# The second feed-forward matrix by a seven-product 2x2 scheme, with the lower halves of the weight sums made by GpSimd

## What is computed

```python
        h = rmsnorm(x, norm_ffn[l])
        x = x + jnp.square(jax.nn.relu(h @ w_ff1[l])) @ w_ff2[l]
    return rmsnorm(x, final_norm)
```

## Time and profile before

| | |
|---|---|
| median of 3 runs | 1634.88 us (1634.79 to 1635.48) |
| span of the profiled execution | 1632.7 us |
| PE busy | 1612.9 us, 99% |
| DVE, ACT, POOL busy | 51%, 51%, 44% |
| mean granted clock of PE | 0.998 of full speed |
| the four passes | from about 526 to 874 us |

### The profile page before, as it was taken

One profiled execution on the slowest core, in us unless ns is written; L12 is line 12 of the kernel. 1 busy time (PEld: TensorE's weight loads), 2 busy tenths in 40 slices (PEclk: granted clock), 3 DMA queues, 4 the chain that ended last, 5 costly groups with the idle time before them and its releaser, 6 DMA issues.

```text
span 1632.7 us, 21256 instructions
## 1 busy us (share of the span) xinstructions
PE 1612.9 (99%) x7503; PEld 1331.9 (82%) x7503; DVE 836.2 (51%) x1278; ACT 828.1 (51%) x1109; POOL 710.5 (44%) x934
## 2 busy tenths in 40 slices
PE   7999999999999999999999999999999999999998
PEld 6888888888888888888887788888888887888886
DVE  3566666632114212121245957447447548688677
ACT  6467777743243413232346645444444446755675
POOL 7453333346666555555566535635635623000000
PEclk9999999999999999999999999999999999999999
DMA  7222221123333333333333222422322323332311
GB/s 209 78 83 60 64 77 58 46 71 110 90 116 91 103 91 103 91 102 92 103 90 90 78 65 77 116 65 75 115 69 65 116 65 92 92 92 69 106 64 62
DMA packets 249048, 142.93 MB, mean 88 GB/s; under 512 B 6162, under 2 KB 245523, under 8 KB 248979
## 3 DMA queue, kind: packets, MB, share of 16 engines
q1 hardware_dynamic: 248978, 142.00, 29.8%
HBM read 139.89 MB, written 2.10 MB: 87 GB/s over the span
## 4 chain that ended last, share of the span: by engine, by line
PE 78%; DVE 1%; issue 0%; ACT 0%; DVEq 0%
PE bank L806 21%; PE bank L807 20%; PE bank L814 20%; PE bank L797 2%; PE bank L799 2%; PE bank L798 2%; PE bank L1131 1%; PE bank L1112 1%; PE bank L1114 1%; PE bank L1113 1%; PE bank L1257 1%; PE bank L1259 1%; PE bank L1258 1%; PE bank L1164 1%; PE bank L1160 1%; PE bank L1162 1%
## 5 line engine op out<-in xcount | busy, mean ns | idle before, releaser
L777 POOL TENSOR_TENSOR w_lo<-raw,w_hi 128x256 fp32r<-128x256 f32 x896 | 699.5, 813 | 652.0 <-ACT w_hi L1364 651.5
L1364 ACT ACTIVATE w_hi<-raw 128x1024 fp32r<-128x1024 f32 x264 | 277.6, 1055 | 499.6 <-PE bank L814 453.6
L806 PE MATMUL bank<-h_hi,w_hi 128*128 128x512 f32 x1252 | 497.1, 397 | 0.0
L807 PE MATMUL bank<-h_lo,w_hi 128*128 128x512 f32 x1252 | 487.9, 390 | 0.0
L814 PE MATMUL bank<-h_hi,w_lo 128*128 128x512 f32 x1252 | 309.8, 389 | 0.0
L806 PEld LDWEIGHTS bank<-h_hi,w_hi 128*128 128x128 f32 x1252 | 235.1, 188 | 54.2 <-issue 6.0
L807 PEld LDWEIGHTS bank<-h_lo,w_hi 128*128 128x128 f32 x1252 | 235.1, 188 | 52.0 <-issue 4.1
L814 PEld LDWEIGHTS bank<-h_hi,w_lo 128*128 128x128 f32 x1252 | 235.0, 188 | 49.3 <-issue 0.5
L2202 DVE TENSOR_TENSOR xT<-xT,bank 128x512 f32<-128x512 f32 x102 | 67.5, 685 | 203.7 <-PE bank L814 159.6
L2227 DVE SCALAR_TENSOR_TENSOR fr<-bank,rstd 128x512 f32<-128x512 f32 x32 | 22.1, 691 | 132.5 <-PE bank L814 126.9
L806 PE MATMUL bank<-f_hi,w_hi 128*128 128x512 f32 x224 | 87.1, 389 | 0.0
(11 more groups left out here) (435 smaller groups left out, 2644.2 us busy)
## 6 DMA issues: line engine op xcount, KB each, us to landing
raw<-in_w_ff SPq DMA_DIRECT2D x64, 512.0 KB, 3.9
raw<-in_w_in SPq DMA_DIRECT2D x56, 512.0 KB, 3.7
raw<-in_m_w_in SPq DMA_DIRECT2D x48, 512.0 KB, 3.9
raw<-in_r_w_in SPq DMA_DIRECT2D x24, 512.0 KB, 3.8
raw<-in_m_w_out SPq DMA_DIRECT2D x16, 512.0 KB, 3.3
raw<-in_r_w_out SPq DMA_DIRECT2D x16, 384.0 KB, 3.0
raw<-in_w_up_b SPq DMA_DIRECT2D x8, 512.0 KB, 4.0
raw<-in_w_out SPq DMA_DIRECT2D x8, 512.0 KB, 4.0
```

Of the source, the lines that this page charges most:

```text
L777: ins = pool.tensor_tensor(w_lo[:, s, part], raw[:, s, part], w_hi[:, s, part].bitcast(F32), ALU.subtract)
L806: pe.matmul(dst, w_hi[:, s, c], hi[:, k, :], start=(k == 0), stop=False)
L807: pe.matmul(dst, w_hi[:, s, c], lo[:, k, :], start=False, stop=False)
L1364: act.activation(w_hi[:, p % RING, :], raw[:, p % RING, :], ACT.Copy).then_inc(hi_ready[p % RING], 1)
```

## The change

The second half of each pass is regrouped. The 2 x 2 blocks are: two output tiles of 128 (tiles 2c and 2c+1, "pair c", c = 0 to 3), two halves of the 1024 hidden units, and two halves of the 512 tokens. The scheme makes the four block products with seven multiplications of sums ("turns") instead of eight, each turn over 4 hidden tiles and 256 tokens.

- **PE** (`pair`): seven turns of 4 x 3 matmuls of 256 columns for each pair of panels, where there were 2 x 24 of 512. Turns add up in a bank (region 0 takes turns 0, 2, 4 and 6), so several values pass through it, and a turn waits until DVE has added the one before (semaphore chain).
- **DVE**: for each pair four weight sums of 128 x 512 in ss (`weight_sums`), made during the pair before it, those of pair 0 in the first half behind tile 4; seven adds of 256 columns from PSUM to xT; and in the first half differences of activation tiles (ft), with the lower halves of seven forms (`forms`). f_hi and f_lo hold seven forms x 4 hidden tiles x 256 tokens.
- **ACT**: per pair w_hi slots 0 (first panel), 1 and 2 (the sums, 1024 columns each) and 3 (half of the second panel), each once the turns that used it are done (`pair_upper`); in the first half the rounded forms in pieces. The copies of pair 0 stand among the squares of tiles 4 to 7: slot 3's comes behind all forms of tile 7.
- **POOL** (`pair_lower`): 14 pieces of 256 columns per pair where it made 8.
- **SP**: the raw slots of a pair are also released by DVE's sums (s_made). The first half's hidden tiles are taken in the order 0, 4, 1, 5, ...
- **The last pass**: the preparation of pair c's two tiles stands on DVE between the adds of pair c+1, one step behind each add; that of pair 3 behind everything. On ACT it stands behind the copies of the next pair's slots, for pair 3 behind the copies of the second block's first four panels.
- Some semaphores elsewhere are merged under new names, and a memset of gone moves from before the last pass to behind it.

```diff
+FORMS = 7
+NC = 4
+TURNS = [(0, 0, 0), (0, 1, 1), (1, 0, 4), (1, 1, 3), (2, 0, 5), (2, 1, 2), (3, 0, 6)]
+REGION = [0, 2, 0, 1, 0, 1, 0]
+CHAIN = 5
...
-        f_hi = sb("f_hi", [P, DT, S], F32R, a)
-        f_lo = sb("f_lo", [P, DT, S], F32R, a)
+        f_hi = sb("f_hi", [P, FORMS, NC, HALF], F32R, a)
+        f_lo = sb("f_lo", [P, FORMS, NC, HALF], F32R, a)
...
+        ft = sb("ft", [P, 4, HALF], F32, a)
+        ss = sb("ss", [P, 2, 4, S], F32, a)
...
+            def pair_lower(i, c):
+                one, two = 2 * c % RING, (2 * c + 1) % RING
+                at = (F_P + 8 + 2 * c) // RING + 1
+                pool.wait_ge(hi_ready[one], i * (F_N // RING) + at)
+                for q in range(PIECES):
+                    part = slice(q * QP, (q + 1) * QP)
+                    ins = lower(0, part, raw[:, one, part])
+                ins.then_inc(lo_ready[one], 1)
+                for s in (1, 2):
+                    pool.wait_ge(sum_hi, i * (2 * NC) + (2 * c + s))
+                    sums = ss[:, c % 2, 2 * s - 2:2 * s, :].rearrange("p a c -> p (a c)")
+                    for q in range(PIECES):
+                        part = slice(q * QP, (q + 1) * QP)
+                        ins = lower(s, part, sums[:, part])
+                        if q % 2:
+                            ins.then_inc(sum_lo_pool, 1)
+                pool.wait_ge(hi_ready[two], i * (F_N // RING) + at)
+                for q in range(2):
+                    part = slice(q * QP, (q + 1) * QP)
+                    ins = lower(3, part, raw[:, two, S + q * QP:S + (q + 1) * QP])
+                ins.then_inc(lo_ready[two], 1)
...
+            with pool.Fori(0, 4) as i:
+                for e in range(8):
+                    panel_lower(e % RING, i * (F_N // RING), (F_P + e) // RING + 1)
+                for c in range(NC):
+                    pair_lower(i, c)
...
+            def pair(i, c):
+                p, t = F_P + 8 + 2 * c, F_T + 8 + c // 2 * RING + c % 2
+                for n, (s, half, form) in enumerate(TURNS):
+                    dst = bank[[c % 2, 2 + c % 2, 5 + c % 2][REGION[n]]][:, 0:HALF]
+                    if n == 0:
+                        bank_ready(t, i, F_N)
+                        panel_split(pe, p, i, F_N)
+                    elif n == 2:
+                        pe.wait_ge(sum_lo_pool, i * (4 * NC) + (4 * c + 1))
+                        pe.wait_ge(chain, i * (CHAIN * NC) + (CHAIN * c + 1))
+                    elif n == 3:
+                        bank_ready(t + 2, i, F_N)
+                        pe.wait_ge(sum_lo_pool, i * (4 * NC) + (4 * c + 2))
+                    elif n == 4:
+                        pe.wait_ge(sum_lo_pool, i * (4 * NC) + (4 * c + 3))
+                        pe.wait_ge(chain, i * (CHAIN * NC) + (CHAIN * c + 3))
+                    elif n == 5:
+                        pe.wait_ge(sum_lo_pool, i * (4 * NC) + (4 * c + 4))
+                        pe.wait_ge(chain, i * (CHAIN * NC) + (CHAIN * c + 4))
+                    elif n == 6:
+                        panel_split(pe, p + 1, i, F_N)
+                        pe.wait_ge(chain, i * (CHAIN * NC) + (CHAIN * c + 5))
+                    for k in range(NC):
+                        if c == 0 and n in (0, 1, 2, 4):
+                            pe.wait_ge(f_made, i * (5 * NC) + (5 * k + {0: 1, 1: 3, 2: 4, 4: 5}[n]))
+                        at = slice(half * S + k * P, half * S + (k + 1) * P)
+                        pe.matmul(dst, w_hi[:, s, at], f_hi[:, form, k, :], start=(k == 0 and n in (0, 1, 3)),
+                                  stop=False, skip_group_check=True)
+                        pe.matmul(dst, w_hi[:, s, at], f_lo[:, form, k, :], start=False, stop=False,
+                                  skip_group_check=True)
+                        mm = pe.matmul(dst, w_lo[:, s, at], f_hi[:, form, k, :], start=False, stop=(k == NC - 1),
+                                       skip_group_check=True)
+                    mm.then_inc(turn_done, 1)
...
+            def pair_upper(i, c, before=None):
...
+                def free(turns, panel):
+                    if c:
+                        act.wait_ge(turn_done, i * (FORMS * NC) + (FORMS * (c - 1) + turns))
+                    else:
+                        tile_full(act, F_P + 4 + panel, i, F_N)
+                        if before:
+                            before(panel)
+                sums = ss[:, c % 2].rearrange("p a c -> p (a c)")
+                free(2, 0)
+                panel_loaded(act, p, i, F_N)
+                act.activation(w_hi[:, 0, :], raw[:, p % RING, :], ACT.Copy).then_inc(hi_ready[p % RING], 1)
+                free(4, 1)
+                act.wait_ge(s_made, i * (4 * NC) + (4 * c + 3))
+                act.activation(w_hi[:, 1, :], sums[:, 0:2 * S], ACT.Copy).then_inc(sum_hi, 1)
...
+                free(7, 3)
+                panel_loaded(act, p + 1, i, F_N)
+                act.activation(w_hi[:, 3, 0:S], raw[:, (p + 1) % RING, S:2 * S], ACT.Copy)\
+                   .then_inc(hi_ready[(p + 1) % RING], 1)
...
+                pair_upper(i, 0, lambda panel: squared(4 + panel))
+                for c in range(NC):
+                    if c + 1 < NC:
+                        pair_upper(i, c + 1)
+                    else:
+                        for panel in range(RING):
+                            act.wait_ge(turn_done, i * (FORMS * NC) + (FORMS * c + [2, 4, 6, 7][panel]))
+                            act.sem_inc(panel_done[panel], 2)
+                            upper(F_P + F_N + panel, i, F_N)
                     if last:
...
+            def weight_sums(i, c):
...
+                def first():
+                    panel_loaded(dve, p, i, F_N)
+                    panel_loaded(dve, p + 1, i, F_N)
+                    if c > 1 or not isinstance(i, int) or i > 0:
+                        dve.wait_ge(sum_lo_pool, i * (4 * NC) + (4 * c - 4))
+                    dve.tensor_tensor(to[:, 1, :], two[:, 0:S], two[:, S:2 * S], ALU.add).then_inc(s_made, 1)
+
+                def second():
+                    dve.tensor_tensor(to[:, 2, :], one[:, 0:S], two[:, 0:S], ALU.subtract).then_inc(s_made, 1)
+                def third():
+                    dve.wait_ge(s_made, i * (4 * NC) + (base_s + 1))
+                    dve.tensor_tensor(to[:, 0, :], to[:, 1, :], one[:, 0:S], ALU.subtract).then_inc(s_made, 1)
+                def fourth():
+                    dve.wait_ge(s_made, i * (4 * NC) + (base_s + 3))
+                    dve.tensor_tensor(to[:, 3, :], one[:, S:2 * S], to[:, 0, :], ALU.subtract).then_inc(s_made, 1)
...
+                def forms(e):
+                    c, z = e // 2, e % 2
+                    dve.wait_ge(ff_made, i * DT + (e + 1))
+                    if z == 0:
...
+                    else:
+                        dve.wait_ge(ft_made, i * (3 * NC) + (3 * c + 1))
+                        dve.tensor_tensor(ft[:, 1, :], ff[:, 1, HALF:S], ft[:, 0, :], ALU.subtract)\
+                           .then_inc(ft_made, 1)
+                        dve.wait_ge(fhi_made, i * DT + (e + 1))
+                        dve.tensor_tensor(f_lo[:, 1:3, c, :], halves_of(ff[:, 1, :]),
+                                          f_hi[:, 1:3, c, :].bitcast(F32), ALU.subtract).then_inc(f_made, 1)
+                        dve.tensor_tensor(ft[:, 2, :], ff[:, 1, HALF:S], ff[:, 0, HALF:S], ALU.subtract)
+                        dve.wait_ge(ft_made, i * (3 * NC) + (3 * c + 2))
+                        dve.tensor_tensor(ft[:, 3, :], ff[:, 1, 0:HALF], ft[:, 1, :], ALU.subtract)\
+                           .then_inc(ft_made, 1)
+                        dve.wait_ge(fthi_made, i * (3 * NC) + (3 * c + 2))
+                        dve.tensor_tensor(f_lo[:, 4, c, :], ft[:, 1, :], f_hi[:, 4, c, :].bitcast(F32),
+                                          ALU.subtract).then_inc(f_made, 1)
+                        dve.wait_ge(fthi_made, i * (3 * NC) + (3 * c + 3))
+                        dve.tensor_tensor(f_lo[:, 5:7, c, :], ft[:, 2:4, :], f_hi[:, 5:7, c, :].bitcast(F32),
+                                          ALU.subtract).then_inc(f_made, 1)
+
+                first, second, third, fourth = weight_sums(i, 0)
                 for e in range(8):
-                    add_x(e, F_P + 8 + e, F_T + 8 + e, i, F_N, F_N)
...
+                    relu(e)
+                    forms(e)
+                    if e == 4:
+                        first()
+                        second()
+                        third()
+                        fourth()
+
...
+                for c in range(NC):
+                    r1, r2, r3 = bank[c % 2], bank[2 + c % 2], bank[5 + c % 2]
+                    x1, x2 = xT[:, 2 * c, :], xT[:, 2 * c + 1, :]
+                    at = FORMS * c
+                    behind = tiles(c - 1) if last and c else iter(())
+
+                    def add(n, x, src, op, sem_):
+                        dve.wait_ge(turn_done, i * (FORMS * NC) + (at + n))
```

(17 more changed lines are left out.)

288 lines of the change are left out of this document (179 added, 109 removed).

## The result

| | before | after |
|---|---|---|
| median | 1634.91 us (1634.79 to 1635.48) | 1653.51 us (1652.84 to 1654.64) |
| ratio | | 1.0114 (95% interval 1.0100 to 1.0129) |
| span of the profiled execution | 1632.7 us | 1651.3 us |
| PE, DVE, ACT, POOL busy | 99, 51, 51, 44% | 98, 60, 53, 49% |
| second halves, passes 0 to 3 | 43.5 each | 44.96, 45.35, 45.35, 54.12 |

The change costs 18.6 us. The page of the changed kernel: busy times and chain, then PE's waits (us in total, times, longest), to be held against the earlier trace rows.

What follows compares the result with a forecast made beforehand. It took GpSimd, held up by VectorE's weight sums, to become the bound over TensorE. 5.4 + 0.7 + 7.8 + 1.9 + 3.1 = +18.9 us on 1634.9 gave 1653.8 us, with an 8-in-10 range of 1642 to 1665.

Steps and rivals of the forecast that it cites:

- its own signs: Wrong if GpSimd's pieces stay 0.7 us beside sums, turn 2 starts before 5 us, or clock drops under 1.00 in passes.
- TensorE's own time: Second half: a turn 1.44 us, a pair 10.08, a half 40.3; 3.2 us less per pass if nothing waits.
- The boundary: Start of second half: turn 2 waits for VectorE's first add, starting at 6.2 us instead of 2.9; 3.3 us lost per pass.
- GpSimd's chain: Second half: GpSimd needs 11.7 us a pair, pair 3 starts at 35.2, half 45.3; +1.8 us in each of passes 0-2.
- The price of 0.455 us per operation: GpSimd time lost per VectorE operation with two SBUF inputs; ends 0.37 and 0.54; enters 68 times.
- Pass 0's extra 0.7: Pass 0: VectorE enters late after waiting for rstd and carries up to 1.4 us to the boundary; 0.7 us added.
- Rival (b): TensorE's clock falls at the boundary, turns 2 and 3 at half speed: 1.7 to 2.9 us per pass, 1661-1665; chance 0.15.
- Rival (a): Second halves: GpSimd keeps ahead, sums cost it less; 1632 us if nothing, 1628 with faster matmuls; chance 0.09.
- (c): TensorE's half-width matmuls don't run in half the time: 0.188 us period, half 63 us, kernel 1713; chance 0.01.
- (d): A sum blocks GpSimd for its whole duration, 0.69 us instead of 0.455: 16 us more, 1670; chance 0.02.
- The last pass: VectorE's six further operations a pair raise GpSimd to 14.4 us: half +7.8, next stage's first lower half +1.9.
- The next stage: Its first panel: late raw panel 3 delays tile 7's h_lo, and column sums wait 0.8 us for VectorE's adds; +3.1 us.

Runs made afterwards that it cites:

- filler: Changed kernel plus 13 unused 256-column matmuls on TensorE in each second half, where turns 1 and 2 of pair 0 wait; 1652.2 us.
- early: Changed kernel with VectorE's first addition of pair 0 right behind the second group of tile 7's forms, pair 1's sums one place later; 1652.9 us.
- dve3: Changed kernel with VectorE instead of GpSimd making slot 3's lower half, leaving GpSimd 12 pieces a pair; 1648.2 us.
- no_sums: Changed kernel without VectorE's four weight sums per pair, only their counts given, so output is not the reference's; 1643.0 us.
- floor: Changed kernel without the weight sums, first addition moved earlier, next stage's tiles 6 and 7 prepared before its panels 2 and 3; wrong output; 1629.7 us.
- no_prep: Changed kernel without all but two of VectorE's operations preparing the next stage in the last pass; output not the reference's; 1644.6 us.
- tail: Changed kernel with ScalarE, in the last pass, preparing tiles 6 and 7 before the next stage's weight panels 2 and 3; 1650.4 us.

## Why the prediction was right, point by point

The median came out 0.3 us from the forecast. That is luck in good part. The sum left out the clock, and by its own signs the prediction was wrong there: the clock row dropped under 1.00 in all four passes (0.50 from 575.5 to 578.5 us, 664.2 to 667.2, 753 to 756 and 842 to 848). With the clock kept up at the boundaries (filler) the halves are 1.1, 1.1, 1.1 and 9.0 us longer than before the change; with the 2.9 of the next stage that makes about 15 us, an estimate, where the sum had 18.9. The fallen clock filled 3.4 of the difference. What was right is the mechanism: VectorE's sums make GpSimd the bound. The terms stand so:

- **TensorE's own time**: right. Turns last 1.44 us wherever nothing waits and the clock is up, a pair 10.08.
- **The boundary**: 3.3 us forecast, 2.96 in pass 1, behind the two waits named (f_lo, then the first addition). It is VectorE's order: with the addition moved, turn 2 starts at 3.80 (early). It would hold the half at 43.6 us by itself, as the text says, and dve3's pass 1 has 43.39 where GpSimd has slack and the clock holds. In the changed kernel GpSimd's chain is the later bound and alone sets pair 3's start.
- **GpSimd's chain**: pair 3 at 35.2 forecast, 35.21 measured, and halves of 45.3 against 45.35. The bound is the one named, but the fit is made of errors that cancel. GpSimd started at 5.15 us and not 5.7; it then waited 0.97 us for a slot that the slow turn 3 let go late, where the text has it busy without a gap; and its 34 pieces and the sums beside them took 28.9 us and not 29.5. Without the slow turns the chain ends at 34.5 (filler). The price of 0.455 us per operation measured 0.48. In the last pass it was 0.54: 15.13 us a pair against 12.97 without sums (no_sums), and that against 9.75 without the preparation too (floor). Pass 0's extra 0.7 did not come: it is 0.4 shorter than the others, not longer.
- **Rival (b)**, at 0.15, happened beside the main case. The clock fell in all four passes, and the slow turns cost 1.58 us in pass 1, just under the 1.7 to 2.9 forecast. What was misjudged is how much of it shows: in passes 0 to 2 most of it fills time that TensorE would have waited in anyway, and 0.4, 0.7 and 0.7 us are left; in the last pass 1.7 are (filler). The half speed in it was an estimate; measured, matmuls stand 0.213 us apart instead of 0.120 in pass 1, where the clock is 0.50. The clock row of 0.52 stands behind 3 us with 0.94 of work, but that such idle time alone brings the clock down is not shown: see dve3's pass 1 in the last section.
- **Rival (a)** did not occur: the sums cost GpSimd 0.48 us each, above the 0.31 at which passes 0 to 2 break even. Where they are left out the scheme wins, as (a) says (floor: 1629.7, with turn 2 early; (a) had 1632 with turn 2 late).
- **Rivals (c) and (d)** did not occur: 0.120 us a matmul, and 0.48 us a sum, not 0.69.
- **The last pass**: forecast 9.7 (7.8 + 1.9), measured 10.6. GpSimd's 14.4 us a pair measured 15.1. The boundary cost 4.05 us there, not 3.3, with 2.7 of slow turns behind it; the sum had neither. Leaving out VectorE's preparation shortens this half by 5.6 us (no_prep), leaving out the sums by 5.3 (no_sums); the two overlap.
- **The next stage**: forecast 3.1, measured 2.87. The parts named in the text, 2.0 behind h_lo and 0.8 at the column sums, come to 2.8. ScalarE's order is what lets them arise (tail).

The sum by measurement: 1.4 + 1.8 + 1.8 + 10.6 + 2.9 = 18.5 us, where 6.1 + 9.7 + 3.1 = 18.9 was forecast.
